# Filler products of a recurrent pair in seven runs instead of twenty

## The reference

```python
def step(state, inp):
    r_t, w_t, k_t, v_t, a_t, b_t = inp
    sa = jnp.einsum("bhij,bhj->bhi", state, a_t)
    state = (state * w_t[:, :, None, :] + sa[..., None] * b_t[:, :, None, :]
             + v_t[..., None] * k_t[:, :, None, :])
    return state, jnp.einsum("bhij,bhj->bhi", state, r_t)
```

## Time and profile before

| | |
|---|---|
| Time of 3 runs, median (lowest to highest) | 3726.64 us (3726.31 to 3728.76) |
| Profiled execution: its own time | 3727.94 us |
| Profiled execution: span of its instructions | 3726.1 us |
| Mean granted TensorE clock | 0.876 |
| TensorE matmul busy | 3063.5 us, 82% |
| TensorE weight loads busy | 2282.0 us, 61% |
| VectorE busy | 1463.0 us, 39% |
| ScalarE busy | 424.8 us, 11% |
| Chain that ended last: PE / DVE / issue / DMA | 65% / 17% / 8% / 5% |

### The profile page before, as it was taken

One profiled execution on the slowest core, in us unless ns is written; L12 is line 12 of the kernel. 1 busy time (PEld: TensorE's weight loads), 2 busy tenths in 40 slices (PEclk: granted clock), 3 DMA queues, 4 the chain that ended last, 5 costly groups with the idle time before them and its releaser, 6 DMA issues.

```text
span 3726.1 us, 51055 instructions
## 1 busy us (share of the span) xinstructions
PE 3063.5 (82%) x22525; PEld 2282.0 (61%) x22525; DVE 1463.0 (39%) x2560; ACT 424.8 (11%) x842; POOL 249.7 (7%) x372
## 2 busy tenths in 40 slices
PE   5997999999954567679979989999997545667798
PEld 4776777777643343347757777777774434333575
DVE  4533454545223652422035226454542256443101
ACT  0001221112011110100000013111210111011000
POOL 5000010000000110010000000100000011000000
PEclk7998999999977558789989989999998765677899
DMA  7862322121322122055458523212214121121352
GB/s 267 318 246 103 119 97 88 63 89 61 103 94 74 52 67 104 24 182 189 161 195 319 203 96 123 95 63 89 68 53 151 68 69 57 52 97 47 123 167 93
DMA packets 224862, 439.94 MB, mean 118 GB/s; under 512 B 7272, under 2 KB 102054, under 8 KB 224640
## 3 DMA queue, kind: packets, MB, share of 16 engines
q1 hardware_dynamic: 210528, 393.49, 30.3%
q0 software_dynamic: 11232, 32.69, 2.8%
q10 hardware_dynamic: 2880, 10.49, 0.7%
HBM read 420.78 MB, written 15.86 MB: 117 GB/s over the span
## 4 chain that ended last, share of the span: by engine, by line
PE 65%; DVE 17%; issue 8%; DMA 5%; ACT 3%; POOL 1%; SPq 0%; DVEq 0%; POOLq 0%; ACTq 0%
PE ps L927 63%; DVE scratch L1706 6%; DVE scratch L1712 5%; DVE scratch L1709 3%; DMA ring<-in_ffn_w 2%; DMA scratch<-acs_scratch 1%; ACT scratch L1627 1%; DVE merged L1905 1%; ACT scratch L1458 1%; DVE hT L1709 1%; DVE scratch L1919 1%; PE ps L1332 1%; DMA ring<-in_w_branch_rwkv 0%; PE ps L1390 0%; DMA ring<-in_w_branch_mamba 0%
## 5 line engine op out<-in xcount | busy, mean ns | idle before, releaser
L927 PE MATMUL ps<-scratch 64*64 64x32 f32 (+6 forms) x14112 | 1123.1, 268 | 168.0 <-DVE scratch L1706 42.1
L927 PE MATMUL ps<-hT,ring 128*128 128x256 f32 (+1 forms) x4992 | 1139.8, 388 | 32.6 <-DVE hT L1709 31.0
L927 PEld LDWEIGHTS ps<-scratch 64*64 64x64 f32 (+2 forms) x14112 | 786.2, 150 | 527.2 <-issue 256.1
L927 PEld LDWEIGHTS ps<-hT,ring 128*128 128x128 f32 (+1 forms) x4992 | 958.9, 194 | 196.2 <-DVE hT L1709 33.2
L1706 DVE TENSOR_TENSOR scratch<-scratch,ps 128x256 f32<-128x256 f32 (+3 forms) x304 | 153.6, 505 | 1089.6 <-ACT scratch L1468 672.9
L927 PE MATMUL ps<-ring,hT 128*128 128x256 f32 (+1 forms) x1664 | 460.3, 416 | 6.6 <-DVE hT L2324 4.9
L927 PEld LDWEIGHTS ps<-ring,hT 128*128 128x128 f32 x1664 | 300.5, 192 | 94.5 <-issue 46.2
L1706 DVE TENSOR_TENSOR scratch<-scratch 128x512 f32<-128x512 f32 (+5 forms) x452 | 306.6, 678 | 65.7 <-DMA scratch<-acs_scratch 20.9
L927 PE MATMUL ps<-ring,scratch 128*128 128x512 f32 x512 | 239.0, 630 | 31.6 <-DMA ring<-in_w_branch_mamba 15.9
L927 PEld LDWEIGHTS ps<-ring,scratch 128*128 128x128 f32 x512 | 103.3, 204 | 164.2 <-issue 139.0
L1712 DVE SCALAR_TENSOR_TENSOR scratch<-ps,prm,scratch 128x254 f32<-128x254 f32 x192 | 92.6, 482 | 235.4 <-ACTq L1630 228.9
(11 more groups left out here) (211 smaller groups left out, 1386.4 us busy)
## 6 DMA issues: line engine op xcount, KB each, us to landing
ring<-in_w_in SPq DMA_DIRECT2D x56, 2048.0 KB, 8.0
ring<-in_ffn_w SPq DMA_DIRECT2D x88, 1024.0 KB, 10.0
scratch<-in_ada_w SPq DMA_DIRECT2D x36, 2048.0 KB, 14.3
scratch<-in_ffn_w SPq DMA_DIRECT2D x44, 1024.0 KB, 5.0
ring<-in_w_branch_mamba SPq DMA_DIRECT2D x8, 2048.0 KB, 7.9
scratch<-acs_scratch POOLq DMA_DIRECT2D x32, 512.0 KB, 4.9
fill_scratch<-scratch ACTq DMA_DIRECT2D x20, 512.0 KB, 7.5
ring<-in_w_branch_rwkv SPq DMA_DIRECT2D x4, 2048.0 KB, 10.4
```

Source lines behind the costliest of these rows:

```text
L927: return pe.matmul(o, lhsT, rhs, start=start, stop=stop)
```

## The change

One table of counts is replaced. In each pair four products more are drawn at each of "ops", "mid" and "lv", three instead of two at "k1", "k3" and "k4", none at "k0" and "k2", and none at the eleven points of the hand-overs. The count at "end" stays at five, and so does the sum per pair: 12 + 8 + 8 + 10 + 11 + 5 = 54 before and 16 + 12 + 12 + 9 + 0 + 5 = 54 after. Since ScalarE reads the same table through `filled`, the units that it empties at each of its points follow.

```diff
--- before.py
+++ after.py
@@ -51,9 +51,9 @@
 
 FILL_BANKS = (1, 7)
 FILL_EARLY = (("vlow", 8), ("vlow_evac", 4), ("vmix0", 4), ("vmix2", 4), ("vmix3", 4), ("kk", 6), ("root", 12), ("rates0", 16), ("rates1", 22))
-FILL_PAIR = (("ops", 12), ("mid", 8), ("lv", 8), ("k0", 2), ("k1", 2), ("k2", 2), ("k3", 2), ("k4", 2),
-             ("r0", 1), ("u0", 1), ("s1", 1), ("r1", 1), ("u1", 1), ("s2", 1), ("r2", 1), ("u2", 1), ("s3", 1),
-             ("r3", 1), ("u3", 1), ("end", 5))
+FILL_PAIR = (("ops", 16), ("mid", 12), ("lv", 12), ("k0", 0), ("k1", 3), ("k2", 0), ("k3", 3), ("k4", 3),
+             ("r0", 0), ("u0", 0), ("s1", 0), ("r1", 0), ("u1", 0), ("s2", 0), ("r2", 0), ("u2", 0), ("s3", 0),
+             ("r3", 0), ("u3", 0), ("end", 5))
 
 
 def filled(p, point):
```

## The result

The changed kernel takes 3770.3 us (median; 3769.4 to 3774.9), the one before 3726.5 beside it: ratio 1.0122, 95% interval 1.0105 to 1.0140. It is slower by 44 us, where 22 were forecast. Its profiled execution took 3774.9 us with a span of 3773.1, 47.0 more than the span before; 45.8 of these lie in the 14 stretches from one pair's bonus product to the next.

A forecast was written before the change was run, and what follows sets the result against it. It took TensorE, holding about two thirds of the chain that ended last, to bound the kernel; 3727.9 + 3.6 at full clock + 19 for clock falls = 3750.5, 1.3 over the median, so 3749 us, range 3720 to 3792.

The forecast's parts named there:

- The mechanism: In the hand-overs without products, TensorE's work gets so thin that its clock falls in nearly every ordinary pair: +19 us.
- this case: Main case: the clock falls in the hand-overs, chance 0.55, own range 3738 to 3768 us.
- full clock: All 16 pairs without new clock losses: 16 x 0.29 less 1 us for first and last pairs, +3.6 us.
- clock losses that begin in levels: Two pairs that already lost the clock behind k3, 6.0 and 2.0 us, were left in unchanged at 8 us.
- The price of one: One clock fall in a pair's hand-overs costs at least 1 us, at most 2.0; 1.6 chosen, for 12 pairs.
- a rival: Clock falls already between k1 and k3, staying low to ops; each pair pays 6.0 us: +92, 3818 us; chance 0.13.
- Hand-over rounds: Hand-overs, j = 0 to 3: a round without products lasts 0.92 us; emptying them gains 3.53 us per pair.
- The rival "covered": At ops and mid, moved products fill waits for VectorE and ScalarE, 1.3 us per pair covered: 3710 us; chance 0.14.
- ScalarE's lora work queues behind nothing new: ScalarE's queue: filler units are emitted earlier than before, so its lora, exponential and gate work is not delayed; cost nothing.
- the net of +0.29: Per ordinary pair at full clock: costs of longer runs 5.91 us against gains in levels and hand-overs 5.62.
- The bounds of the full-clock sum: Over all pairs: +13 us with no cover at mid and less gained; -18 with shorter waits and cover at lv.
- rule on long idle gaps: Skill page asks only for no long idle gap; by it the clock holds in hand-overs: 3730 us, chance 0.18.

The follow-up runs named there:

- experiment 3: Changed kernel plus four extra unused products in the idle stretch ahead of j = 2's r block: 3741.6 us; control, the same four ahead of j = 1: 3793.1 us.
- the levels alone: Kernel before with k0 and k2 emptied, three products at k1, k3, k4, nine at lv, hand-over products kept: 3716.4 us, ratio 0.9978.
- experiment 2: Kernel before with the eleven hand-over products moved to ops, mid and lv (16, 12, 11), two kept at each of k0 to k4: 3788.2 us, ratio 1.0164.

## Why the prediction was wrong

The mechanism, the place of the main loss and the sign were right; the size was not: 3770.3 lies just past even the range of 3738 to 3768 that was given for this case. The 14 ordinary stretches add up to 879.4 us before and 925.2 after. Their difference of 45.8, term by term beside the forecast:

| | forecast | measured |
|---|---|---|
| full clock | +3.6 | 14 x (62.54 - 61.96) = +8.1 |
| clock losses in hand-overs | 12 x 1.6 = +19 | 14, +34.8 in all |
| clock losses that begin in levels | as before, 8 | 2 again, but 14.8 |
| extra time of five other pairs before, not counted above | none | -3.9 |

(34.8 is 925.2 less 14 x 62.54 less 14.8, and so holds the extra time of other pairs after; 14.8 is what the pairs of 70.3 and 71.1 have over 63.2 and 63.4, other pairs of the short kind. The -3.9 is the other time that the stretches before have over 14 x 61.96, beside the two losses of 8.0; half of it is one pair whose lead-in ran at the lower level for 3.4 us. 8.1 + 34.8 + 14.8 - 8.0 - 3.9 = 45.8.)

- **The step that failed:** "The price of one: at least 1 us [...], at most the 2.0 of the shorter loss; 1.6 chosen". A pair without a loss takes 62.54, most of the short kind 63.2 to 63.7, most of the long kind 66.1 to 66.8: prices of about 0.7 to 1.2 and of 3.6 to 4.2, half and half, 2.5 on average. Where the long one goes can be read from the rows: from the r block of j = 2 to the y block 7.81 us (789.05 to 796.86), where the pair without a loss of experiment 3 takes 5.98; y and turn 1.48 (796.86 to the end run at 798.34) against 0.85; the end products 3.44 against 2.26. Together 3.6. The two blocks there:

```profile
842.91 0.68 PE L927 MATMUL ps<-scratch 64*64 64x64 f32 x16 [0.45 <-DVE scratch L1712]
848.89 0.45 PE L927 MATMUL ps<-scratch 64*64 64x64 f32 x8 [0.60 <-DVE scratch L2047]
```

  I took the upper bound from the shorter of the two losses before. The pair of 68.0 had shown one that lasts, and I used it only for a rival. The short and the long kind have the same work behind the scan, so that work alone does not set how long a loss lasts; what does is not shown.
- **The count** was 14 and not 12: every pair with a scan in its hand-overs, none of those without.
- **Losses in the levels** were to cost what they had. Their number stayed at two; their price nearly doubled: before, the clock was low for 13.7 and 3.4 us, after for 17.1 us each time, and why longer stays open. The prediction put them down to the piece behind k3 as the longest without a product, and overlooked what stands just ahead of both, and ahead of the two after as well: an idle stretch of TensorE that an ordinary pair does not have there. The first two of these rows are of the kernel before, the others of the changed one, where the losses begin in the piece between k1 and k3:

```profile
695.75 0.80 PE L927 MATMUL ps<-scratch 64*64 64x32 f32 x16 [0.48 <-DVE scratch L1706]
2668.32 0.59 PE L927 MATMUL ps<-scratch 64*64 64x32 f32 x14 [0.23 <-issue]
2499.43 3.21 PE L927 MATMUL ps<-scratch 64*64 64x32 f32 x74 [0.40 <-issue]
2696.35 7.27 PE L927 MATMUL ps<-scratch 64*64 64x32 f32 x156 [0.35 <-issue]
```

  The clock falls 0.4 to 2.2 us later. Three of the four end with "issue": the profile shows nothing that TensorE waited for. Not every such stretch is followed by a loss (one of 0.55 us in the four-product kernel of experiment 3 is not), and no run here adds or removes one, so the link is not shown.
- **Hand-over rounds:** 0.91 us measured against 0.92. The last pair's chain gave 3.85 us; the ordinary one (hand-overs to turn 15.10 us in experiment 3, 18.24 before) gave 3.14 where 3.53 was worked out.
- **Runs at ops, mid and lv:** 7.00, 5.38 and 5.38 us against 5.27, 4.22 and 3.65, so +1.73, +1.16, +1.73 as worked out, and no cover found beyond that at mid. The rival "covered" falls. In the levels -0.9 against -0.8.
- **"ScalarE's lora work queues behind nothing new"** was true and missed the point. Nothing stands in front of it, but the rounds r and u of j = 1 got shorter, while its four activations did not: VectorE's rates wait 0.46 us for them. This takes most of what the hand-overs gained less, and with it the net of +0.29 becomes the +0.58 measured. It costs some 4 to 6 us.
- **The bounds of the full-clock sum** do not follow from their terms: 16 x (0.29 - 0.60 - 0.57) - 1 is -15 and not -18, and 16 x (0.29 + 0.57 + 0.20) - 1 is at least +16 and not +13. Neither enters the forecast or its range.
- **The page of the Trainium skill** ("TensorE: Matmul & The Clock Gate", "Why this matters for your kernels"): by its rule on long idle gaps nothing should have fallen. The runs decide against it as a sufficient rule: gaps of 2.37 us lost the clock in 14 of 14 pairs, of 1.94 us in 12 and of 1.30 us in 5, in the midst of 64-row blocks, where the last pair's 0.81 did not.
- **That runs cost something in themselves** held too: 61.50 us with the levels alone, from three runs instead of five. The Trainium skill, "TensorEngine Tiling (Array Packing)", section "Key Properties", says that a change of tiling mode drains the array; the 0.2 us per run agrees with it, though no run here separates this from other costs of a run.

## What to carry to other kernels

Filler work between two waits has two uses, and a count of its cost at full clock sees only one: it also keeps up TensorE's clock. Before it is taken out of a thin chain, look where the longest idle gap will then be, and put filler into just that gap; there it is free as long as it does not reach past the wait (here 61.96 to 60.37 us per pair). And a clock loss is not to be priced by the shortest one seen: the same code here lost 0.7 to 1.2 us in one pair and 3.6 to 4.2 in the next.

## What was not expected of the hardware

- The two lengths of pairs take turns (63.7, 66.2, 63.2, 66.3 in the first layer; with one product in the gap 66.4, 63.3, 66.4, 63.3, 66.4, 63.3 in the second) though instructions and work are the same. What decides whether a loss is short or long is not shown.
- One of four executions of the kernel with one extra product took 6189.9 us, and it was the one profiled; the others took 3753 to 3760. VectorE's busy time is what it always is, but matmuls take as long as they do at the lower level or a little longer (128 records of 32 columns 7.52 us, where the worst pair of experiment 2 has 7.04 at clock 0.50). The table of stretches still reads 1.00 for that part, because the trace holds no clock record ahead of 4483 us; from there on it reads 0.52 to 0.55:

```profile
1246.93:1359.96 113.03, 112.28 (x925) 83.83 (x924) 30.85 (x73) 7.69 (x17) 3.20 (x5) 1.00 0.15 49
4483.00:5000.00 517.00, 500.79 (x4511) 351.22 (x4511) 143.22 (x343) 42.87 (x83) 13.42 (x20) 0.54 0.14 47
```

A clock of 1.00 in the table is therefore to be checked against the duration of a known matmul. Why the execution was slow is open; it did not happen again, and nothing above rests on it.
